# The output projection's 512-column products written as pairs of 256 columns

## The reference

```
p = rmsnorm(x) @ w_in[l]     -> mixer a | mixer b | mixer c | cross-attention q | gate
mixer:  layer 0  softmax attention in a band of 9 chunks of 64 tokens
        layer 1  gated linear recurrence, computed in blocks of 64 (here 128) tokens
cross:  4-head attention into 256 memory tokens
y = concat(mixer_out, cross_out) * silu(gate)
x = x + y @ w_out[l]
```

## Time and profile before

| what | value |
|---|---|
| median of three executions | 2377.52 us |
| the profiled execution, first to last instruction | 2376.1 us |
| PE busy | 2312.2 us, 97% of the span, 23787 matmul records |
| weight loads busy | 2094.7 us, 88% |
| DVE, ACT, POOL busy | 77%, 59%, 16% |

### The profile page before, as it was taken

How to read it: one execution, slowest core, us unless ns; L and a number is a source line. 1 busy time by engine, 2 the same in 40 slices (tenths; PEclk the granted TensorE clock), 3 DMA queues, 4 the chain that set the end, 5 groups by cost and what they waited for, 6 DMA issues and landing times. The chain is left out here.

```text
span 2376.1 us, 61711 instructions
## 1 busy us (share of the span) xinstructions
PE 2312.2 (97%) x23787; PEld 2094.7 (88%) x23787; DVE 1819.5 (77%) x3555; ACT 1413.5 (59%) x3281; POOL 381.0 (16%) x585
## 2 busy tenths in 40 slices
PE   7999999999989999999999999999999989999998
PEld 4999999999967888888887999999999978888886
DVE  7889788887666656666666998797888777888885
ACT  4564666755565555555554564776757566666664
POOL 2332000000022221211112332000000112112111
PEclk9999999999999999999999999999999999999999
DMA  6886887769894222222226897886879793444442
GB/s 227 298 299 219 301 281 231 247 220 332 232 307 121 83 66 89 90 69 83 73 81 232 272 303 242 256 275 214 266 248 312 230 269 117 129 131 122 137 135 70
DMA packets 396664, 469.64 MB, mean 198 GB/s; under 512 B 39860, under 2 KB 248556, under 8 KB 396376
## 3 DMA queue, kind: packets, MB, share of 16 engines
q1 hardware_dynamic: 379832, 406.02, 54.4%
q0 software_dynamic: 14704, 54.92, 6.6%
q10 hardware_dynamic: 1840, 4.75, 0.7%
HBM read 318.77 MB, written 151.56 MB: 198 GB/s over the span
## 5 line engine op out<-in xcount | busy, mean ns | idle before, releaser
L1468 PE MATMUL pj_acc<-x_lo,pj_wh 128*128 128x256 f32 (+1 forms) x3080 | 780.9, 284 | 0.0
L1468 PE MATMUL pj_acc<-x_hi,pj_wh 128*128 128x256 f32 (+1 forms) x3080 | 780.8, 284 | 0.0
L1468 PEld LDWEIGHTS pj_acc<-x_hi,pj_wh 128*128 128x128 f32 x3080 | 578.4, 188 | 0.0
L1468 PEld LDWEIGHTS pj_acc<-x_lo,pj_wh 128*128 128x128 f32 x3080 | 578.4, 188 | 0.0
L509 ACT ACTIVATE pj_wh<-pj_wt 128x512 fp32r<-128x512 f32 x676 | 420.3, 634 | 255.9 <-DMA pj_wt<-tsum 175.1
L516 DVE SCALAR_TENSOR_TENSOR pj_wl<-pj_wt,pj_wh 128x512 fp32r<-128x512 f32 x676 | 467.0, 708 | 87.0 <-ACT pj_wh L509 79.3
L1464 PE MATMUL pj_acc<-x_hi,pj_wl 128*128 128x256 f32 (+1 forms) x3080 | 509.4, 287 | 13.8 <-DVE pj_wl L516 11.9
L1464 PEld LDWEIGHTS pj_acc<-x_hi,pj_wl 128*128 128x128 f32 x3080 | 425.3, 188 | 22.1 <-DVE pj_wl L516 19.5
L1307 DVE TENSOR_TENSOR pj_out<-pj_out,pj_acc 128x512 f32<-128x512 f32 (+1 forms) x448 | 320.8, 716 | 103.3 <-PE pj_acc L1468 69.7
L2541 DVE COPY pb_pt<-pb_SCTP 128x256 f32<-128x256 f32 (+2 forms) x266 | 115.8, 435 | 147.5 <-PE pb_SCTP L2352 74.3
L2676 ACT ACTIVATE pb_se<-pb_se,pb_mn 128x640 f32<-128x640 f32 (+4 forms) x208 | 154.6, 745 | 114.6 <-DVE pb_mn L2524 114.3
(11 more groups left out here) (371 smaller groups left out, 3992.1 us busy)
## 6 DMA issues: line engine op xcount, KB each, us to landing
pj_wt<-tsum SPq DMA_DIRECT2D x546, 256.0 KB, 3.8
proj<-pj_out SPq DMA_DIRECT2D x112, 512.0 KB, 4.2
tsum<-pj_wt SPq DMA_DIRECT2D x140, 256.0 KB, 3.2
pj_wraw<-in_w_in_dram POOLq DMA_DIRECT2D x24, 1024.0 KB, 6.6
tsum<-pj_wraw SPq DMA_DIRECT2D x56, 256.0 KB, 4.2
hg_x<-x_mid SPq DMA_DIRECT2D x17, 512.0 KB, 3.7
pb_gate<-proj SPq DMA_DIRECT2D x16, 512.0 KB, 5.1
pb_x<-in_x_prompt_dram SPq DMA_DIRECT2D x16, 512.0 KB, 3.8
```

The source lines that it names most:

```text
L1468: ins = nc.tensor.matmul(BANK[j][:, 0:n], w.hi[j][:, k], x.of(y, p, j)[:, k], start=False, stop=(k == 3 and i == 1))
```

## The change

In both mixers the product of 512 columns becomes two matmuls of 256 columns, on columns 0 to 255 and 256 to 511 of the same bank, with the same stationary operand. The start flag stands only on the first matmul of a bank, and the stop flag and the semaphore only on the last. In the recurrent mixer the three products are now written as a loop, with their waits where they were. Nothing else changes, in particular no DMA and no instruction of another engine.

```diff
-                        cs = slice(half * 512, half * 512 + 512)
-                        ins = nc.tensor.matmul(sum_of(job, half), (yl if part == 2 else yh)[job % 2][:, k],
-                                               (wol if part == 1 else woh)[:, group_of(job, k), cs],
-                                               start=(k == 0 and part == 0), stop=(k == KD - 1 and part == 2))
+                        for at in (0, 256):
+                            cs = slice(half * 512 + at, half * 512 + at + 256)
+                            ins = nc.tensor.matmul(sum_of(job, half)[:, at:at + 256], (yl if part == 2 else yh)[job % 2][:, k],
+                                                   (wol if part == 1 else woh)[:, group_of(job, k), cs],
+                                                   start=(k == 0 and part == 0 and at == 0), stop=(k == KD - 1 and part == 2 and at == 256))
...
-                        cs = slice(half * 512, half * 512 + 512)
                         g = GROUPS[s]
-                        nc.tensor.matmul(to[:], yh[:, s], woh[:, g, cs], start=(s == 0), stop=False)
-                        nc.tensor.matmul(to[:], yh[:, s], wol[:, g, cs], start=False, stop=False)
-                        if s % 4 == 0:
-                            pe.wait_ge(s_yl, 2 * job + s // 4 + 1)
-                        ins = nc.tensor.matmul(to[:], yl[:, s], woh[:, g, cs], start=False, stop=(s == KD - 1))
+                        for part, (a, b) in enumerate(((yh, woh), (yh, wol), (yl, woh))):
+                            if part == 2 and s % 4 == 0:
+                                pe.wait_ge(s_yl, 2 * job + s // 4 + 1)
+                            for at in (0, 256):
+                                cs = slice(half * 512 + at, half * 512 + at + 256)
+                                ins = nc.tensor.matmul(to[:, at:at + 256], a[:, s], b[:, g, cs],
+                                                       start=(s == 0 and part == 0 and at == 0), stop=(s == KD - 1 and part == 2 and at == 256))
```

## The result

| | before | after |
|---|---|---|
| median of the executions, us | 2381.19 (2376.17 to 2387.34, 5) | 2397.74 (2393.91 to 2404.81, 5) |
| the profiled execution's span, us | 2376.1 | 2396.0 |
| mean granted clock | 0.997 | 0.995 |

The ratio is 1.007, with a 95% interval from 1.0049 to 1.009: the kernel became slower by about 16.6 us, where 10.5 us less were forecast. The median lies well above the range. (The median of before is higher than the 2377.52 us of the first three executions, because two more were added beside the new kernel.)

The account below looks back on a forecast made before the run. PE's own stream was taken to bound both mixers. Savings of 6.8 us (band) and 4.3 us (recurrent), less 0.6 us of issue waits, gave −10.5 us: median 2367.0 us, range 2361 to 2378.

Parts of the forecast that it names:

- third rival: Recurrent mixer: shorter products no longer hide DVE and ACT steps between levels; 2370.7 us, or 2374 to 2377; chance 0.15.
- The fixed 0.33: Ends of product runs, both mixers: if scores always start 0.33 us after the last product's start, 14 us lost; little weight.
- The price of a product of 256 columns: Both mixers: a half costs 0.1133 us as in the layer-0 projection, a pair 0.2267, less than one 512-column product.
- the line through 320 and 512 columns: Upper bound for a half in both mixers: 0.119 us, pair 0.238, +7 us in all.
- the surplus (7, 14, 19): Nanoseconds above columns over 2.4 GHz at 256, 320 and 512 columns; two halves pay 13, one product 19 to 22.
- first rival: Both mixers: a half costs more than in the projection, over 0.1168 us on average; +7.3 us, 2385 us; chance 0.09.
- The 235 ns: Band mixer: price taken for a 512-column product, from a period of five transposes and three products; saving there 6.8 us.
- The rule from the Trainium skill: Any warm matmul: columns over 2.4 GHz plus fixed 2.5 ns, so splitting loses 4 us over 1632 products; not followed.
- grow with the instructions: Recurrent mixer: 5.2 us of issue waits in runs of tiny matmuls grow by 11%, costing 0.6 us.
- second rival: Recurrent mixer's level runs: PE runs out of instructions, 0.6 us per added wait, 18 cancel the saving; 2380 us; chance 0.04.
- the sum: Both mixers: 6.8 plus 4.3 us saved, less 0.6 us of issue waits, net −10.5; half-price bounds −16.2 to +7 us.

Follow-up runs that it names:

- price_list: Kernel before plus blocks of 16 products after its work, quiet and beside SBUF or PSUM copies: 512 columns 0.233 us, a half 0.118; total time not meaningful.
- price_loads: Kernel before plus quiet blocks with moved operand starts and narrower weights: 256 columns cost 117.1 ns with 64 weight columns, 117.3 with 32, 118.1 with 128.
- spare_waits: Kernel before plus five long-met waits ahead of each recurrent-mixer product, 1734 more PE instructions: 2401.69 us against 2383.55, ratio 1.0085.

## Why the prediction was wrong

**Right.** PE is the engine that sets both mixers; the clock stayed at its upper level (0.99 to 1.00 of 2.4 GHz in the windows); 816 matmuls and loads came to each mixer and nothing else moved. The projections kept their time, and PE's waits for other engines did not grow (3.2 us in the recurrent mixer before, 2.1 after), so the third rival had nothing to it. The exposed end of a run is unchanged: scores follow the last product of 512 columns after 0.327 us and the last half after 0.209, which is 0.09 more than a product's pace in both (as measured over 64 such ends of the band mixer). The fixed 0.33 that I weighed and left aside is refuted.

**The step that failed first: "The price of a product of 256 columns."** It took 0.1133 us from the projection, where it is typical (the median step of 256 columns there is 113 ns), and passed over the line through 320 and 512 columns, which it named itself with 0.119. Measured are 0.118 in runs, against 0.2327 for the product. The step had noticed that the surplus (7, 14, 19) bends oddly and used it all the same; in blocks of the kernel's own tiles the surplus of 256 columns is 11 to 12, more than half of the 20. As a term: the band mixer was to gain 6.8 us and lost about 3.1; the recurrent mixer was to gain 4.3 and lost 3.9 in its products, 2.7 of it (816 × 3.3 ns) by the usual price. That is a swing of some 18 us. The first rival's condition (over 0.1168 us) came true, and its price of +7.3 us is near the 7.0 found. Both reasons that it gave are refuted, traffic by `price_list`, the load's cover by `price_loads`. The evidence against it was worth nothing: a lower price in a busier stretch does not tell what these tiles cost. The 235 ns for a product of the band mixer was too high as well: behind one another its products started 233 ns apart, as in the other mixer.

The rule from the Trainium skill, TensorE: Matmul & The Clock Gate, section "Back-to-back issue gap", that two matmuls pay the fixed part twice, had the sign right and I set it aside. The section gives it for an isolated matmul, and about 131 ns for one of 512 columns in a stream, which no run here comes near. The rule's sizes do not fit this kernel either: it gives 109 ns for 256 columns and 216 for 512, measured are 118 and 233; its difference of a pair from a product, 2.5 ns, is a little under the 3 to 5 found.

**The second: the issue waits, "grow with the instructions by 816/7517 = 11%, so 0.6 us".** They grew by 8.5 us, from 5.1 to 13.6. Proportion was the wrong rule for something that arises where a supply is just not enough. The second rival had the mechanism and the bound of 18 more gaps. There were eight more, and the mean gap was longer (0.8 us against 0.6); four of the seventeen stand in the products, where it had not looked and where there was one before. Eleven lie within lines 2992 to 3002, one more than the ten it had named as the limit. Its evidence against, that pairs use half the rate of tiny matmuls, was misread: pairs come at 8.5 matmuls a us, and those of a level at about ten times that (92 records in 1.09 us in the kernel after). `spare_waits` shows that no added matmul is needed for it. Alone the 8.5 us would have left −2.6 us of the forecast's saving. The recurrent mixer's 12.4 us are then 3.9 for the products, 8.5 for issue waits and −1.1 for waits on other engines, 11.3 in all; about 1 us more lies in the steps around the gaps, which the overlap of records does not let me divide.

**The chances.** The two rivals had 0.09 and 0.04 as though they excluded each other, and each was to eat up the whole saving alone. They are independent, and both came. The range ended under the upper bound of the cost that the sum had named as unknown, at +7 us; it should have reached it.

**Left open.** Whether the projection's 0.1133 comes from its offsets, what makes the offsets matter, and why the gaps double. None of the kernels tried is faster than before.

## What to carry to other kernels

Price a new shape in the tiles and the stretch where it will stand, by neighbours in width there, and treat one row from another stage as one sample; a single wide matmul is the safer choice where the column price is nearly in proportion. Count an engine's instructions, waits included, wherever it also runs hundreds of tiny ones, and look for idle time called issue that ends behind an instruction packet: here such time did not grow in proportion. When an unknown price has bounds on both sides of no change, let the range reach both.

## What the runs showed of the hardware beyond that

- The price of an fp32r matmul depends on where its operands start within 128 bytes: 227 to 234 ns for 512 columns, 115 to 120 ns for 256 (113 once settled, in one block), and within 2 ns not on the width of its weights (32, 64 or 128 columns) or on copies running beside it.
- Instructions reach PE in packets of 16384 bytes, 256 instructions each (49454 in 193 packets before, 52718 in 206 after). Where they come late, PE goes on 1.2 to 1.7 us after the landing as a rule.
- Waits that are long met are not free: 1734 such instructions made the kernel 0.85% slower (0.72 to 0.99).
